# A two-model transformer kernel: the RWKV tail in shifted halves with wide products between, X joined by block transposition, GpSimd's subtractions in pieces

## The reference, cut to what matters

```
def step(state, inp):
    r_t, w_t, k_t, v_t, a_t, b_t = inp
    sa = jnp.einsum('bhvk,bhk->bhv', state, a_t)
    state = (state * w_t[:, :, None, :] + sa[..., None] * b_t[:, :, None, :]
             + v_t[..., None] * k_t[:, :, None, :])
    return state, jnp.einsum('bhvk,bhk->bhv', state, r_t)
...
y = rwkv7_scan(rh, heads(decay), kh, vh, -kk, kk * ah)
...
bonus = jnp.sum(rh * kh * r_k.astype(jnp.float32), axis=-1, keepdims=True) * vh
out = (y + bonus.reshape(B, S, RW_DIM)) * g
```

## Time and profile before

| | |
|---|---|
| median of 3 runs | 4059.29 us (4054.79 to 4061.07) |
| the profiled execution's own time | 4055.24 us |
| its span | 4053.5 us |
| PE busy | 3873.0 us, 96% |
| DVE, ACT, POOL busy | 1954.3, 1635.8, 1652.3 us |
| mean granted TensorE clock | 0.975, and 1.00 in the stretches of the pairs |

### The profile page before, as it was taken

How to read it: one execution, slowest core, us unless ns; L and a number is a source line. 1 busy time by engine, 2 the same in 40 slices (tenths; PEclk the granted TensorE clock), 3 DMA queues, 4 the chain that set the end, 5 groups by cost and what they waited for, 6 DMA issues and landing times. The chain is left out here.

```text
span 4053.5 us, 67108 instructions
## 1 busy us (share of the span) xinstructions
PE 3873.0 (96%) x28244; PEld 3167.8 (78%) x28244; DVE 1954.3 (48%) x3042; ACT 1635.8 (40%) x2723; POOL 1652.3 (41%) x902
## 2 busy tenths in 40 slices
PE   8999989999999899998899999989999999999998
PEld 6888867878887788886787888777878887787887
DVE  7777673246534777767324654436231123523112
ACT  5554444343334555444434333446233224523222
POOL 4444412434445444441243444534444444444443
PEclk9999999989999899999998999989999999999999
DMA  3111113325532211111332554221222322122332
GB/s 134 48 49 44 67 45 112 104 99 188 186 131 98 85 48 49 44 68 44 111 99 97 193 183 135 99 73 43 98 89 99 98 90 79 53 94 89 99 99 83
DMA packets 108731, 379.52 MB, mean 94 GB/s; under 512 B 12561, under 2 KB 12945, under 8 KB 107793
## 3 DMA queue, kind: packets, MB, share of 16 engines
q1 hardware_dynamic: 98208, 357.27, 25.9%
q10 hardware_dynamic: 10224, 17.97, 1.2%
HBM read 359.46 MB, written 15.73 MB: 93 GB/s over the span
## 5 line engine op out<-in xcount | busy, mean ns | idle before, releaser
L293 POOL TENSOR_TENSOR Wlo<-raw,Whi 128x1024 fp32r<-128x1024 f32 x552 | 1334.4, 2420 | 1995.2 <-ACT Whi L280 1995.0
L228 PE MATMUL ps<-hh,Whi 128*128 128x512 f32 x2864 | 1152.1, 402 | 27.9 <-DVE hl L377 10.1
L228 PE MATMUL ps<-hl,Whi 128*128 128x512 f32 x2864 | 1123.4, 392 | 0.0
L228 PE MATMUL ps<-hh,Wlo 128*128 128x512 f32 x2864 | 1123.2, 392 | 0.0
L280 ACT ACTIVATE Whi<-raw 128x1024 fp32r<-128x1024 f32 x552 | 581.8, 1055 | 708.9 <-PE ps L228 607.9
L228 PEld LDWEIGHTS ps<-hh,Whi 128*128 128x128 f32 x2864 | 542.7, 189 | 160.2 <-issue 28.3
L228 PEld LDWEIGHTS ps<-hl,Whi 128*128 128x128 f32 x2864 | 543.1, 190 | 116.7 <-issue 8.6
L228 PEld LDWEIGHTS ps<-hh,Wlo 128*128 128x128 f32 x2864 | 542.2, 189 | 115.8
L228 PE MATMUL ps<-gh,Whi 128*128 128x512 f32 x864 | 337.6, 391 | 3.8 <-POOL Wlo L293 3.8
L228 PE MATMUL ps<-gh,Wlo 128*128 128x512 f32 x864 | 336.2, 389 | 0.0
L228 PE MATMUL ps<-gl,Whi 128*128 128x512 f32 x864 | 336.1, 389 | 0.0
(11 more groups left out here) (363 smaller groups left out, 5913.6 us busy)
## 6 DMA issues: line engine op xcount, KB each, us to landing
raw<-in_stream SPq DMA_DIRECT2D x554, 512.0 KB, 3.5
ada<-in_ada SPq DMA_DIRECT2D x96, 512.0 KB, 4.6
park_x<-xT SPq DMA_DIRECT2D x2, 2048.0 KB, 7.3
park_yh<-yh ACTq DMA_DIRECT2D x16, 256.0 KB, 2.1
park_yl<-yl ACTq DMA_DIRECT2D x16, 256.0 KB, 2.3
xT<-park_x SPq DMA_DIRECT2D x2, 2048.0 KB, 8.8
yrh<-park_yh ACTq DMA_DIRECT2D x16, 256.0 KB, 8.0
yrl<-park_yl ACTq DMA_DIRECT2D x16, 256.0 KB, 7.9
```

Of the source, the lines that this page charges most:

```text
L228: last = pe.matmul(ps, left[a](k), right[c](k), start=start and k == 0 and i == 0, stop=stop and k == n - 1 and i == 2)
L293: pool.tensor_tensor(b["Wlo"][:, slot], b["raw"][:, raw_slot(b, u)], b["Whi"][:, slot].bitcast(F32), SUB) \
```

## The change

1. **X by block transposition.** The 16 matmuls of level 0 that turn XT, and ACT's two copies to X, are gone. DVE adds `Wc = TM + identity` (128x256) per head, and transposes it in 32x32 blocks into `X`. The mask of level 0 joins only neighbouring rows, so blocks of 32 hold it all.
2. **The tail.** U of head 0; a quarter of r; U of head 1 interleaved chunk by chunk with Z of head 0; quarter 0 of k; Z of head 1 interleaved with L of head 0; quarter 1; L of head 1; quarter 2; then M as before. Quarter 3 stands after S3, and none after S2.
3. **The levels.** After levels 1, 2 and 3 one quarter of r each, where r had two halves after 1 and 2 and k its first quarter after 3. ACT empties the bank of r in the tail after U of head 0.
4. **DVE's order.** In the tail S2 comes right after RY of head 0, S3 right after RY of head 1, and the two copies to `y` last. The bonus of the pair before stands ahead of `rwkv_prep1_dve` and not behind it.
5. **POOL's pieces.** The `low_parts` in the pairs (four units a pair) are done in four instructions of 128x256 each. Elsewhere it stays one of 128x1024.

```diff
+LOW_PIECES = 4
-def low_parts(pool, s, b, first, end):
+def low_parts(pool, s, b, first, end, pieces=1):
...
+        for i in range(pieces):
+            part = slice(i * UNIT // pieces, (i + 1) * UNIT // pieces)
+            last = pool.tensor_tensor(b["Wlo"][:, slot, part], b["raw"][:, raw_slot(b, u), part], b["Whi"][:, slot, part].bitcast(F32), SUB)
+        last.then_inc(s["w_lo"], 1)
...
-    for h in range(2):
-        pe.wait_ge(s["inv_v"], INV_V(p, f"T0{h}"))
-        for c in range(BLK):
-            for u in range(2):
-                last = pe.matmul(b["ps"][half(1 - u), 4 + h, block(c)], b["XT"][half(u), h, block(c)], b["c"]("identc")[half(u)],
-                                 start=True, stop=True)
-        last.then_inc(s["inv_p"], 1)
...
+    for c in range(BLK):
+        u_part(0, c)
+    if p + 2 < PAIRS:
+        rwkv_gemm_pe(pe, s, b, ring, p + 2, "r", 3, 4)
+    else:
+        early_query_pe(pe, s, b, ring, FILL[p, "r"], 3, 4)
+    pe.wait_ge(s["inv_v"], INV_V(p, f"T{LEVELS - 1}1"))
+    pe.wait_ge(s["tail_a"], TAIL_A(p, "U0"))
+    for c in range(BLK):
+        u_part(1, c)
+        z_part(0, c)
+    ahead(0)
+    pe.wait_ge(s["tail_a"], TAIL_A(p, "Z0"))
+    for c in range(BLK):
+        z_part(1, c)
+        l_part(0, c)
     ahead(1)
+    pe.wait_ge(s["tail_a"], TAIL_A(p, "Z1"))
+    for c in range(BLK):
+        l_part(1, c)
+    ahead(2)
...
-        ahead(c + 1)
+        if c == 2:
+            ahead(3)
...
-        act.activation(b["X"][:, h], b["ps"][:, 4 + h, 0:BLK * CB], ACT.Copy).then_inc(s["inv_a"], 1)
...
+            if x == "U" and h == 0:
+                if p + 2 < PAIRS:
+                    rwkv_ev_act(act, s, b, p + 2, "r")
...
+        dve.tensor_tensor(blocks(b["Wc"][:, h]), blocks(b["TM"][:, h, 0]), ident, ADD).then_inc(s["inv_v"], 1)
+    for h in range(2):
+        dve.wait_ge(s["inv_v"], INV_V(p, f"i{h}"))
+        dve.transpose(b["X"][:, h], b["Wc"][:, h]).then_inc(s["inv_v"], 1)
...
-            if l <= 2:
+            if l <= 3:
                 if p + 2 < PAIRS:
-                    rwkv_gemm_pe(pe, s, b, ring, p + 2, "r", l - 1, 2)
+                    rwkv_gemm_pe(pe, s, b, ring, p + 2, "r", l - 1, 4)
...
+            if l == 1 and p:
+                rwkv_bonus_dve(dve, s, b, p - 1)
             if p + 1 < PAIRS:
...
-                low_parts(pool, s, b, u, u + 1)
+                low_parts(pool, s, b, u, u + 1, LOW_PIECES)
```

More of the change, by code:

```diff
@@ L731, in rwkv_inv_pe @@
             pe.wait_ge(s["inv_g"], INV_G(p, f"m{l}{h}"))
[L732 to L735, removed]
+            pe.wait_ge(s["inv_v"], INV_V(p, f"X{l - 1}{h}"))
             for c in range(BLK):
@@ L762, in ahead @@
             early_query_pe(pe, s, b, ring, FILL[p, "k"], part, 4)
[L764 to L784, removed]
+    def u_part(h, c):
+        for u in range(2):
+            last = pe.matmul(b["ps"][half(u), BANK_U + h, c * P:(c + 1) * P], b["XT"][half(u), h, block(c)],
+                             b["AG"][half(u), c, h], start=c == 0, stop=u == 0, skip_group_check=True)
+        if c == BLK - 1:
+            last.then_inc(s["tail_p"], 1)
@@ new lines, in z_part, with l_part @@
+    def z_part(h, c):
+        last = pe.matmul(b["ps"][half(1), BANK_Z + h, c * P:(c + 1) * P], b["TB"][half(0), h, c, 0, CB:P],
+                         b["Wm"][half(0), h, c], start=True, stop=True)
+        if c == BLK - 1:
+            last.then_inc(s["tail_p"], 1)
+    def l_part(h, c):
+        last = pe.matmul(b["ps"][half(1), BANK_U + h, c * P:(c + 1) * P], b["XT"][half(1), h, block(c)],
+                         b["Zs"][half(1), h, c * P:(c + 1) * P], start=False, stop=True, skip_group_check=True)
+        if c == BLK - 1:
+            last.then_inc(s["tail_p"], 1)
@@ L938, in rwkv_tail_act @@
             act.activation(dst[half(u), h], b["ps"][half(u), bank + h], ACT.Copy).then_inc(s["tail_a"], 1)
+            if x == "U" and h == 0:
+                if p + 2 < PAIRS:
+                    rwkv_ev_act(act, s, b, p + 2, "r")
+                else:
+                    early_query_act(act, s, b, FILL[p, "r"])
     act.wait_ge(s["tail_p"], TAIL_P(p, "N"))
@@ L1105, in rwkv_inv_pool @@
                 if l >= 2:
-                    pool.wait_ge(s["inv_p"], INV_P(p, f"W{l - 2}{h}") if l > 2 else INV_P(p, f"X0{h}"))
+                    pool.wait_ge(*((s["inv_p"], INV_P(p, f"W{l - 2}{h}")) if l > 2 else (s["inv_v"], INV_V(p, f"X0{h}"))))
             pool.tensor_tensor(blocks(b["TM"][:, h, l % 2]), blocks(b["TD"][:, h]), lvl[:, l].broadcast_to([P, BLK, CB]), MUL)                 .then_inc(s["inv_g"], 1)
@@ L1146, in rwkv_tail_dve @@
         dve.tensor_tensor(chunks(b["RY"][half(h)]), chunks(ps[half(h)]), b["ar"][half(h), q, :, 1], ADD).then_inc(s["tail_v"], 1)
[L1147 to L1152, removed]
+        state(h + 1, f"S{h + 2}")
+    if p:
+        dve.wait_ge(s["post_v"], POST_V(p - 1, "yl"))
+    for h in range(2):
+        dve.tensor_copy(b["y"][vhalf(h)], b["ps"][vhalf(h), BANK_RY + h]).then_inc(s["tail_v"], 1)
     if p + 1 < PAIRS:
@@ L1324, in between @@
                     rwkv_prep_act(act, s, b, p + 1)
-                if p + 2 < PAIRS:
-                    rwkv_ev_act(act, s, b, p + 2, "r")
-                else:
-                    early_query_act(act, s, b, FILL[p, "r"])
             if l == 3:
@@ L1388, in between @@
                     rwkv_prep1_dve(dve, s, b, p + 1)
-            if l == 1 and p:
-                rwkv_bonus_dve(dve, s, b, p - 1)
             if l == 2 and p:
```

24 lines of the change are left out of this document (9 added, 15 removed).

## The result

The changed kernel took 4084.26 us (median of 4 runs, 4081.90 to 4086.23), the kernel before on the same chip 4059.85 us (4 runs). The ratio is 1.0070, with a 95% interval from 1.0058 to 1.0082: slower, and above the range of 4042 to 4078. The profiled execution had a span of 4081.1 us, 27.7 more than before.

A forecast was written before the change was run, and what follows sets the result against it. PE bounds the kernel now, but DVE, taking turns with POOL, was to decide after the change: 14 pairs at +0.6 us and two last pairs at -2.1 give +4.4, a median of 4064 us, own range 4052 to 4075, wider range 4042 to 4078.

The forecast's parts named there:

- The sum: Whole run: 14 pairs at +0.6 us and two last pairs at -2.1 give +4.4 us, a median of 4064.
- The rule of turns: DVE and POOL: each SBUF-only DVE instruction meeting POOL's queue pays the rest of one POOL instruction; 0.56 to 0.60 us.
- DVE's sum: DVE in a pair, taken to decide: kkr ends at 210.5, PE resumes level 3 at 214.7, 2.7 of 4.0 us lost.
- the estimate beside it: DVE's two transpositions priced from the skill's bf16 figure: 0.6 us for 256 columns, making DVE's sum 5 us more.
- PE's own sum: PE per pair: -1.25 for XT's turning, -2.77 in the levels, +1.9 in the tail, together -2.1 us.
- a pair becomes 0.6 us longer: Pairs preparing a next one: 1.3 us left after level 3's wait, against the tail's +1.9; 14 x 0.6 = +8.6 us.
- The last pair of each layer has no `kkr`, and gives -2.1 twice: Last pair of each layer: without kkr, it gains PE's full 2.1 us, twice.
- B: Rival: DVE's queue is a microsecond shorter, two turns fewer, kkr at 209.3; 4048 us; chance 0.22.
- C: Rival: PE stays the bound, kkr before 207.8, nearly all 34 us come; 4030 us; chance 0.10.
- D: Rival: the tail's mixed phases run one after the other, 1.76 us a pair, +28; 4092 us; chance 0.08.
- E: Rival: the transpositions cost the upper bound, 0.8 us in DVE's queue, +11; 4075 us; chance 0.12.

The follow-up runs named there:

- e2: Changed kernel, but in a layer's last pair ACT makes no high part of one more weight unit after level 5; 4078.46 us, ratio 1.0056.
- e4: Changed kernel with the bonus sum on DVE back behind rwkv_prep1_dve; 4087.10 us, ratio 1.0076.
- e3: Changed kernel with POOL's products whole again (LOW_PIECES = 1); 4109.38 us, ratio 1.0132.
- e6: Kernel before with only X by block transposition on DVE, POOL's products whole; 4097.24 us, ratio 1.0097.
- e1: Changed kernel with ACT's four exponentials ahead of the square of kkr; 4049.71 us, ratio 0.9984.
- e5: Changed kernel with ACT's exponentials ahead of kkr's square, and in last pairs no high part ahead of U's copy; 4043.96 us, ratio 0.9968.
- e9: Changed kernel with ACT's exponentials first, without ACT's wait in last pairs, and X turned by PE and copied by ACT; 4047.41 us, ratio 0.9977.
- e10: Kernel before with three more squares of kkr on ACT for each next pair; 4073.76 us, ratio 1.0041.
- e11: Changed kernel with ACT's exponentials first, without ACT's wait in last pairs, and low part of next k behind level 5; 4036.84 us, ratio 0.9947.
- e8: Changed kernel with X turned by PE and copied by ACT as before, the rest kept; 4071.27 us, ratio 1.0038.
- e7: Changed kernel with the mixed phases apart: Z written behind U's end, L behind Z's; 4089.99 us, ratio 1.0092.
- e12: Changed kernel with the low part of the next pair's k made by POOL behind level 5, not level 3; 4097.49 us, ratio 1.0098.
- e13: Kernel before with five more squares of kkr on ACT for each next pair; 4121.88 us, ratio 1.0165.

## Why the prediction was wrong

The sum stood at 4.4 us for the span and 27.7 came. By its own steps:

- **The rule of turns, and DVE's sum: right.** `kkr` was forecast at 23.0 and came at 22.9, level 1's W at 13.7 and came at 13.7 (205.19 - 191.47), the transpositions 0.4 each and took 0.76 together (the 0.6 each of the estimate beside it, from a figure for bf16, did not come), scans of 0.5 and more, and were 0.88 to 0.95. PE was to go on at level 3 27.2 us after the front (214.7) and did at 26.96; of the 2.7 us of waiting, 1.82 are idle time there and 0.64 at level 2.
- **PE's own sum: right where it was free.** The mixed phases were forecast at 1.02 and took 1.03 and 1.02. The tail was to grow by 3.4 us from U to M and to shrink by 1.48 behind it. In a regular pair (p = 3) it is 10.44 us from U to M where it was 7.02, so 3.4, and 8.52 from M to the next front where it was 10.04, so 1.52.
- **"a pair becomes 0.6 us longer": right,** 0.55 in the regular pairs. But it was multiplied by 14. The two first pairs, whose preparation is another, have longer waits and cost 1.9. With the rounding of the regular pairs that is 1.8 us of the miss.
- **"The last pair of each layer has no `kkr`, and gives -2.1 twice": wrong, +0.8 twice,** 5.8 us of the miss. It has no `kkr`, but two other waits. PE comes to X sooner, because there is no next pair's low-rank work, and waits there, so that 0.15 us of the 1.25 are gained; and ACT's `Whi`, queued by position, waits for a product that the change moved behind the copy it blocks (1.84). Run e2 took that one away. The prediction took over PE's sum for this pair and looked at no other engine's queue in it.
- **The missing term: the clock, 12 us,** half of the miss. The step that failed is "the sum" itself: it priced the new gap at level 3 by its length alone. All the rows for PE's prices were taken at full clock, and nothing asked what a gap does to the products behind it. The run with the exponentials first took gap and falls away together, and the runs with more squares made them by a gap in the old kernel. The other 3.8 us lie outside the pairs, and about 3 of them are clock as well.

Of the rivals none was what happened. B, C and D are refuted (`kkr` at 22.9, a gap, no phases one after the other), and E as well, since the transpositions cost what the forecast says.

The prediction could have known of the clock. The trace of the kernel before shows a fall in one of two passes through the attention stage, which runs once in each layer with the same instructions behind the same gap. PE ahead of it in the second layer, and the windows of that stretch in both layers:

```profile
1865.87 1.88 PE L1490 MATMUL ps<-zr,const 128*128 128x512 f32 x4
1869.72 0.39 PE L228 MATMUL ps<-Whi,hh 128*128 128x256 f32 x1 [1.97 <-ACT zr L1566]
```

```profile
552.70:566.80 14.10, 13.54 (x102) 12.40 (x103) 10.21 (x8) 4.94 (x8) 6.65 (x3) 1.00 0.11 38
1869.90:1885.40 15.50, 14.94 (x102) 13.80 (x104) 10.04 (x8) 4.79 (x8) 6.46 (x3) 0.89 0.10 35
```

A gap of 2.56 us (2.55 in the first layer), and 1.4 us more in the one where the clock fell (1.5 if both are counted from the first product behind the gap, at 552.67 and 1869.72). In the changed kernel it was the other way round, a fall in the first layer and none in the second. Over all fifteen traces this gap was followed by a fall in 11 of 30 passes, so one pass of before could hint at the risk and not price it.

The Trainium skill (TensorEngine Tiling (Array Packing), Key Properties) was quoted ahead for the drain at a change of the tiling mode. The rows of after agree: six wide matmuls between two narrow phases take 234.07 to 235.67, 1.60 us, as the earlier trace rows have 1.59, where six in a run take 1.39.

## What to carry to other kernels

Price a new wait of TensorE not only by its length: read from the trace whether gaps of that length are followed by a lower granted clock elsewhere in the program, and if so add a range for it, from none to every pass, since the place counts as well as the length. Work taken from TensorE in front of a wait that it does not set is not only worth nothing, it lengthens the gap, and that can cost more than the work did: first take away the wait (here an order of ACT's instructions, worth 35 us), then the work. Sum a loop's first and last pass by themselves, over the queues of all engines, since what covers a wait in the others may be missing in them.

## What the runs showed of the hardware

**The clock falls behind a gap, not always, and not at once.** Pairs in which the granted clock fell, by the length of PE's longest gap at level 3 or later, one trace for each kernel (worked out from the traces; in e4 the gap stands ahead of the mean product at level 2; e3 and e6, which have a second gap at level 2, left out):

```
gap 1.2 us or less at level 3 and on (before, e1, e5, e9, e10, e11): 0 of 82
gap 1.70 (e8):                                                      4 of 11
gap 2.01 to 2.06 (after, e2, e4, e7, first pairs of e8):           17 of 50
gap 2.22 (e12):                                                     6 of 12
gap 2.30 (e13):                                                    11 of 12
gap 2.46 to 2.56 (first pairs of after, e2, e4, e7, e10, e12):     11 of 12
gap 3.87 (first pairs of e13):                                      2 of 2
```

A fall costs about 1.5 us or a multiple of it. All 75 falls within the pairs of the fifteen traces start between 0.9 us before and 2.2 us after the end of a gap of 1.4 us or more. So no fall came without a gap, but it is not the gap's length alone that decides. In e12 all six are in the first layer and none in the second, with the same gap of 2.22. In the two kernels left out, the gaps of 2.03 us (e3, level 3) and 2.04 us (e6, ahead of the mean product) had a fall behind them in 8 of 10 and 8 of 12 passes. At these places the clock fell much more rarely:

```
wait at level 2, 1.86 to 1.91 (first pairs of after, e1, e2, e4, e5, e7):    0 of 12
wait at level 2, 2.52 to 2.54 (e3):                                          2 of 12
wait ahead of U of head 1, 2.16 to 2.18 (last pairs, seven kernels):         2 of 14
```

What decides between two such passes stays open.

**DVE and POOL take turns** when both work on SBUF: an instruction of DVE waits out the rest of one of POOL's (it took 2.55 us, its wait included, behind a whole product, and 0.85 to 0.95 behind a piece or a mask), scans as well, while the inverse's additions that read PSUM took 0.39 to 0.42 us in every run.

**TensorE runs a later product of a free quadrant** beside earlier ones of another (e7: Z's first product starts at 233.30, between U's, which run to 233.61 and on).
